# Heads 2 to 6 in couples of seven half products, with the operands kept in DRAM in between

## What is computed

```python
def layer(x, ...):
    h = rmsnorm(x, g_pre_mix)
    z = h @ w_in
    b_g, c_g, xin, cq, ckv_raw, kpe_raw, ga, gb = split(z)
    yc, new_buf = short_conv(c_g * xin, conv_buf, conv_w)
    y_a = b_g * yc
    q = (rmsnorm(cq, g_q) @ w_uq)           # 8 heads, rotary part apart
    y_b = mla_attention(q, latents, rotary keys, w_uk, w_uv)
    merged = sigmoid(ga) * y_a + sigmoid(gb) * y_b
    x = x + rmsnorm(merged @ w_o, g_post_mix)
    f = square(relu(rmsnorm(x, g_pre_ffn) @ w1)) @ w2
    return x + rmsnorm(f, g_post_ffn)
```

## Time and profile before

| | us |
|---|---|
| median of 3 runs | 1749.77 (1749.56 to 1752.14) |
| the profiled execution | 1752.92 |
| its span on the core | 1751.1 |
| TensorE busy in it | 1736.5 (99%) |
| VectorE, ScalarE, GpSimd busy | 1156.4 (66%), 794.3 (45%), 167.9 (10%) |
| mean TensorE clock granted | 0.998 |

### The profile page before, as it was taken

One profiled execution on the slowest core, in us unless ns is written; L12 is line 12 of the kernel. 1 busy time (PEld: TensorE's weight loads), 2 busy tenths in 40 slices (PEclk: granted clock), 3 DMA queues, 4 the chain that ended last, 5 costly groups with the idle time before them and its releaser, 6 DMA issues.

```text
span 1751.1 us, 31636 instructions
## 1 busy us (share of the span) xinstructions
PE 1736.5 (99%) x12975; PEld 1723.4 (98%) x12975; DVE 1156.4 (66%) x2232; ACT 794.3 (45%) x1541; POOL 167.9 (10%) x239
## 2 busy tenths in 40 slices
PE   9999999999999999999999999999999999999998
PEld 9999999999999999999999999999999999999997
DVE  7765555658798566657687555556577886666565
ACT  7634343335465454435366343434345545444452
POOL 0322222000000000000003222222000000000000
PEclk9999999999999999999999999999999999999999
DMA  4688878432213434333227887887513214333331
GB/s 175 174 197 178 192 176 186 106 100 76 86 52 110 131 123 133 121 116 132 74 95 157 168 159 176 148 176 155 135 62 109 74 67 164 120 116 119 126 110 55
DMA packets 83904, 224.57 MB, mean 128 GB/s; under 512 B 9776, under 2 KB 21296, under 8 KB 83760
## 3 DMA queue, kind: packets, MB, share of 16 engines
q1 hardware_dynamic: 57520, 163.82, 28.5%
q0 software_dynamic: 24960, 56.64, 19.3%
q10 hardware_dynamic: 1280, 2.10, 0.4%
HBM read 218.65 MB, written 60.49 MB: 159 GB/s over the span
## 4 chain that ended last, share of the span: by engine, by line
PE 97%; DMA 2%; DVE 1%; ACT 0%; SPq 0%; issue 0%; DVEq 0%
PE ring L720 20%; PE ring L722 20%; PE ring L721 20%; PE att L720 11%; PE att L722 11%; PE att L721 11%; PE att L2992 1%; DMA w_raw<-blocks_in 1%; DMA small_raw<-small_in 1%; PE att L715 1%; PE att L714 1%; PE att L727 0%; PE att L728 0%; PE att L2807 0%; PE att L3048 0%; DVE last L2761 0%
## 5 line engine op out<-in xcount | busy, mean ns | idle before, releaser
L720 PE MATMUL ring<-xs_hi,w_lo 128*128 128x288 f32 x2272 | 674.9, 297 | 0.9 <-issue 0.4
L722 PE MATMUL ring<-xs_hi,w_hi 128*128 128x288 f32 x2272 | 669.2, 295 | 0.0
L721 PE MATMUL ring<-xs_lo,w_hi 128*128 128x288 f32 x2272 | 669.0, 294 | 0.0
L720 PEld LDWEIGHTS ring<-xs_hi,w_lo 128*128 128x128 f32 x2272 | 426.7, 188 | 3.3 <-issue 0.8
L721 PEld LDWEIGHTS ring<-xs_lo,w_hi 128*128 128x128 f32 x2272 | 426.9, 188 | 1.6
L722 PEld LDWEIGHTS ring<-xs_hi,w_hi 128*128 128x128 f32 x2272 | 426.6, 188 | 0.0
L1800 DVE TENSOR_TENSOR w_lo<-w_raw,w_hi 128x1024 fp32r<-128x1024 f32 (+1 forms) x286 | 330.5, 1167 | 73.3 <-ACT w_hi L1270 60.5
L722 PE MATMUL att<-f_hi,w_hi 128*128 128x288 f32 x960 | 283.2, 295 | 0.0
L721 PE MATMUL att<-f_lo,w_hi 128*128 128x288 f32 x960 | 282.9, 295 | 0.0
L720 PE MATMUL att<-f_hi,w_lo 128*128 128x288 f32 x960 | 282.6, 294 | 0.0
L721 PEld LDWEIGHTS att<-f_lo,w_hi 128*128 128x128 f32 x960 | 180.4, 188 | 0.0
(11 more groups left out here) (297 smaller groups left out, 2727.9 us busy)
## 6 DMA issues: line engine op xcount, KB each, us to landing
w_raw<-blocks_in SPq DMA_DIRECT2D x211, 512.0 KB, 4.3
weight_sums<-blocks_in POOLq DMA_DIRECT2D x192, 256.0 KB, 6.8
w_raw<-weight_sums SPq DMA_DIRECT2D x48, 512.0 KB, 3.8
w_raw<-blocks_in SPq DMA_DIRECT2D x26, 256.0 KB, 3.3
weight_sums<-weight_sums POOLq DMA_DIRECT2D x24, 256.0 KB, 6.3
small_raw<-small_in SPq DMA_DIRECT2D x16, 320.0 KB, 4.7
small_raw<-small_in SPq DMA_DIRECT2D x32, 128.0 KB, 5.9
x<-x_in SPq DMA_DIRECT2D x8, 288.0 KB, 6.8
```

The costliest lines, as they stand in the source:

```text
L720: pe.matmul(out, w[1], x[0], start=first, stop=False)
L721: pe.matmul(out, w[0], x[1], start=False, stop=False)
L722: return pe.matmul(out, w[0], x[0], start=False, stop=last)
```

## The change

Heads 2 to 6 ("mixed") no longer make gb, ga, C and x as blocks. C and x form one couple, ga and gb another, each of seven half products (Winograd's form of Strassen, as in the feed-forward couples) over four tiles: x's upper and lower features by both halves of the tokens. B stays a block. A mixed head takes eight slot positions of weights instead of five, two half products each.

For that x is multiplied by its row norm and gain in heads 0 and 1 (`normed_rows`), stored in DRAM (`h_kept`), four differences of it are made over x and `my` (`head_mix`, `head_mix_lo`), and normed x is read back and split in head 2. As `my` is taken, each head's result is stored in `my_kept`, and rows 0 to 6 are read back at head 7, with x (from the input, or in layer 1 from `x_kept`, stored when the layer begins). GpSimd makes the sums of both layers, 44 couples, in one stretch in layer 0, pipelined over four couples.

```diff
+FIRST_MIXED, LAST_MIXED = 2, 6
 # SP
             sp.wait_ge(pl.row_sum, 2 * L + 1)
+            if L > 0:
+                sp.wait_ge(pl.x_new, x_new(L - 1, "post_b", KC - 1))
+                sp.dma_start(pl.x_kept, pl.x[:, :, :]).then_inc(pl.x_spilled, 16)
             sp.dma_start(pl.cos[:, :], tables[0]).then_inc(pl.tables_landed, 16)
             sp.dma_start(pl.sin[:, :], tables[1]).then_inc(pl.tables_landed, 16)
...
+            for h in range(HEADS):
+                if h > 0:
+                    sp.wait_ge(pl.merged, L * HEADS + h)
+                    sp.dma_start(pl.my_kept[:, h - 1, :], my_row(pl, h - 1)).then_inc(pl.my_stored, 16)
+                if h == 1:
+                    sp.wait_ge(pl.h_made, KC * (L + 1))
+                    sp.dma_start(pl.h_kept, pl.x[:, :, :]).then_inc(pl.h_stored, 16)
+                if h == HEADS - 1:
+                    sp.wait_ge(pl.my_stored, stored(L, HEADS - 2))
+                    sp.dma_start(pl.my[:, 0:KC - 1, :], pl.my_kept[:, 0:KC - 1, :]).then_inc(pl.my_landed, 16)
+                    sp.dma_start(pl.x[:, :, :], x_in if L == 0 else pl.x_kept).then_inc(pl.x_back, 16)
+                for j in range(HEAD_POS[h + 1] - HEAD_POS[h]):
+                    if j == (3 if is_mixed(h) else 2):
+                        next_small(h)
...
+                    elif is_mixed(h):
+                        sp.wait_ge(pl.ring_full, full(L, r_mixed(h, (1, 3, 5, 8, 9, 11, 13, 15)[j])))
+                    else:
+                        sp.wait_ge(pl.ring_full, full(L, r_hd(h, j, 1)))
+                    pos_load(HEAD_POS[h] + j + N_HEAD)
 # GpSimd
+        def all_sums():
+            n_sums = DEPTH * (2 * MIXED + PAIRS)
+            sums_copy(0)
+            for n in range(n_sums + 2):
+                if n < n_sums:
+                    pool.wait_ge(pl.sums_copied, 48 * (n + 1))
+                if 1 <= n <= n_sums:
+                    pool.wait_ge(pl.sums_first, 32 * n)
+                if 2 <= n <= n_sums + 1:
+                    pool.wait_ge(pl.sums_second, 16 * (n - 1))
+                if n >= 3:
+                    pool.wait_ge(pl.sums_third, 16 * (n - 2))
+                if n + 1 < n_sums:
+                    sums_copy(n + 1)
+                if n < n_sums:
+                    sums_add_first(n)
+                if 1 <= n <= n_sums:
+                    sums_add_second(n - 1)
+                if n >= 2:
+                    sums_add_third(n - 2)
...
             key_rope(L, 1)
-            for g in range(FIRST_PAIR, GROUPS):
-                for p in range(2):
-                    weight_sums(L, g, p)
+            if L == 0:
+                all_sums()
 # VectorE, a plain head, after the two copies of ga
+                if first:
+                    normed_rows(0, 3)
+                elif h == FIRST_MIXED - 1:
+                    head_mix(0)
+                    head_mix(1)
                 row_maxima(h)
                 absorbed_lo(h, pl.u)
+                if h == FIRST_MIXED - 1:
+                    head_mix(2)
...
                 merge(h, slice(0, NP_), pl.merged)
+                if first:
+                    normed_rows(3, KC)
+                elif h == FIRST_MIXED - 1:
+                    head_mix_lo(2)
+                    head_mix_lo(3)
 # TensorE
+            def mixed_head(h):
+                if h == FIRST_MIXED:
+                    projections(h)
+                for i in range(4):
+                    product(h, 0, i)
+                if h != FIRST_MIXED:
+                    projections(h)
+                for i in range(4, 7):
+                    product(h, 0, i)
+                scores(h)
+                mixed_block(h)
+                turns(h)
+                for i in range(3):
+                    product(h, 1, i)
+                attended(h)
+                for i in range(3, 7):
+                    product(h, 1, i)
```

More of the change, by code:

```diff
@@ L824, in _ @@
                 slot_load(L, n_head(0, i), SLOT_HD[i])
[L825 to L847, removed]
@@ L966, in _ @@
     def _(pool):
[L968 to L986, removed]
@@ L1384, in x_hi_a @@
+            for h in range(HEADS):
+                if is_mixed(h):
+                    mixed_head(h)
+                else:
+                    plain_head(h)
             def x_hi_a(k):
                 if k < HEADS - 1:
[L1386 removed]
+                    eng.wait_ge(pl.my_landed, 16 * (L + 1))
                 else:
@@ new lines, in absorbed_lo, with probabilities @@
+            def absorbed_lo(h, rest):
+                eng.wait_ge(pl.abs_hi, of_head(h, 1, 0))
+                to = slice(64 * h, 64 * (h + 1))
+                rest = rest[:, 0:2 * NS_].rearrange("p (c q) -> p c q", c=CC)
+                own.step(minus(rest, absorbed_tile(pl)[:, :, 0, :], pl.qah[:, :, to]))
+                own.wait()
+                dve.tensor_tensor(pl.qal[:, :, to], absorbed_tile(pl)[:, :, 1, :], rest, ALU.add) \
+                    .then_inc(pl.abs_lo, 1)
+            def probabilities(h):
+                eng.wait_ge(pl.exped, of_head(h, 4, KT - 1))
+                own.step(dve.reciprocal(pl.ri[:, :], pl.rs[:, :]))
+                own.wait()
+                for t in range(KT):
+                    tile = pl.probs[:, PO[t]:PO[t] + P * (t + 1)]
+                    dve.tensor_scalar(tile, tile, pl.ri[:, t:t + 1], None, ALU.mult).then_inc(pl.normed, 1)
@@ new lines, in half_weight, with half_product @@
+            def half_weight(h, n):
+                hi, lo, _ = pl.half_slot(pos_slot(HEAD_POS[h] + n // 2), n % 2)
+                return hi, lo
+            def half_product(idx, weight, x_of, first, last):
+                for k in range(4):
+                    w = slice(k * P, (k + 1) * P)
+                    ins = mm3(pe, pl.ring[:, bank(L, idx), 0:NH], (weight[0][:, w], weight[1][:, w]), x_of(k),
+                              first and k == 0, last and k == 3)
+                return ins
```

1171 lines of the change are left out of this document (785 added, 386 removed).

## The result

The changed kernel took **1902.0 us** (median of 4 runs, 1898.26 to 1913.32), the kernel before 1749.66 beside it: a ratio of 1.088 (95% interval 1.083 to 1.0927), 152 us slower. The forecast was 1758.6 us, between 1732 and 1798. The sign was right, which says little, since the prediction's own chances were 0.49 for slower and 0.40 for faster; the size was off by 143 us. The profiled execution took 1898.26 us, span 1896.4.

What follows compares the result with a forecast made beforehand. TensorE's matmuls were taken as the bound (busy 1736.5 of 1751.1 us). Terms -31.7 + 4.6 + 4 + 6 - 1.1 + 12 + 15 = +8.8 gave 1761.7 us profiled, 1758.6 as median; range 1732 to 1798.

Steps and rivals of the forecast that it cites:

- Removed work: Heads 2 to 6, both layers: couples of seven half products instead of eight remove 240 matmuls, -31.7 us.
- (a): VectorE in a mixed head: about 37 us of 44, staying under TensorE's time, costed at nothing.
- (b): Head 1 of each layer: two differences of x on VectorE ahead of the mask fill, +4.6 us for both.
- (c): Head 2 of each layer: remainders, reloaded normed x and rotary work come together, +4 us for both, bounds 0 and 10.
- (e): Loads beside the sums land late in layer 0's heads 3 to 6, +6 us (0 to 20); layer 1 gains 1.1.
- the faster rival: Loads keep their cover and TensorE stays the bound: 1735 us, between 1728 and 1746; chance 0.36.
- (f): Head 7: reload of result rows and x delays small weights and key cache in layer 0, +12 us (3 to 26).
- (g): Start of layer 1: store of x lengthens the path and key rotation waits behind all sums, +15 us (4 to 45).
- (d): Weight sums on GpSimd: 44 couples, 352 transfers, end at 921 to 972 us, engines about nine tenths full through layer 0.
- the one with the DMA engines as the bound: Rival: DMA engines bound layer 0, sums take until 972 us, 87.5 us of pauses, 1805 us; chance 0.12.
- the bank rival: Half products turn PSUM banks twice as fast, TensorE waits 1 us per couple (20), 1755 us; chance 0.06.

Runs made afterwards that it cites:

- without sums: Changed kernel with all sums of weight blocks left out, plain blocks read instead, so results are not the reference's: 1740.46 us (one run).
- after: The complete changed kernel as first measured, against the kernel before: 1902.0 us median, ratio 1.088.
- the run in two parts: Changed kernel with 32 couples of sums made in layer 0 and the last 12 behind layer 1's key rotation: 1798.66 us median, ratio 1.029.
- The run with less room: Changed kernel with room for GpSimd's queued transfers cut from 1024 to 768 bytes a partition: 1990.64 us.

## Why the prediction was right and wrong, step by step

- **Removed work, -31.7: right.** 240 matmuls fewer. The rate at full clock is the same.
- **(a) VectorE in a mixed head, nothing: right as long as the weights come in time.** Without sums TensorE's waits at products into `ring`, whatever they were for, come to 1.9 us, and to 5.8 in after, not counting one of 1.5 us at the very start that the kernel before has too.
- **(b) head 1, +4.6: right in cause and size.** 2.35 + 2.36 without sums, gone when the calls are moved. In after layer 0's was 5.7, the sums having made the weight block ahead of it late as well.
- **(c) head 2, +4: right.** 3.6 us of pauses in layer 0 (157 to 170 us) and 1.7 in layer 1.
- **(e) late loads, +6: right as far as it went.** 3.0, 2.3 and 1.1 us at 188, 231 and 334 us. But 6.0 us more came in the feed-forward part (1.8, 1.2 and 2.9 at 560, 652 and 843 us), where the sum has no term, though I had written that the engines would be nine tenths full there. That the first sum would be there in time, as the faster rival has it, was wrong: SP stood 17.8 us for it. The 1.1 us of layer 1 are gone, as said.
- **(f) head 7, +12: right in size, and by the reload, but not by the load that I named.** 13.9 us in layer 0, 2.9 in layer 1, where I had nothing. I had the key cache late, ahead of the output projection; ScalarE in fact waited 14.2 us for a weight block behind the reload (issued 388.82, landed 407.62), ahead of the transposes.
- **(g) start of layer 1, +15: wrong, it was 115** (104.2 + 13.2 - 2.4). Its mechanism, the key rotation behind all sums, is what happened, and the run in two parts shows it. The part that I gave to the store of x, 4 us alone and some 11 beside the sums, measures 2.0 without sums (4.3 or 4.4 against 2.4) and 10.8 beside them (13.2 against 2.4): too large alone, right beside the sums. Whose it is stays open, as said above.
- **(d) is the term that failed.** It gave GpSimd's end as 921 to 972 us; it was 1071. I built it from engine time: 352 transfers at 1.40 to 1.69 us of all engines, plus SP's loads, plus 1.5 us idle a round, as if GpSimd's queue got whatever SP leaves free. The run with less room and the round at 1008 us show otherwise. With SP loading nothing, the engines were 0.61 busy and a round still took 21.5 us. The row that had the answer is a start time in the kernel before:

```profile
59.66 0.71 POOL L974 DMA_DIRECT2D weight_sums<-blocks_in  x1
...
300.00 0.83 POOL L974 DMA_DIRECT2D weight_sums<-blocks_in  x1
```

  Eleven couples from the first to the twelfth start: 240.3 / 11 = 21.9 us a couple, with nine transfers and the engines 0.81 busy. 44 x 21.85 from 59.6 on ends at 1021 us, already 93 us past the 928 at which the rotation was due. I took it that eight transfers, with the couples overlapped, would go faster; they took 22.6.
- **What I left out: the clock.** Stretches after long pauses ran below the 2.4 GHz level: the granted clock is 0.86 from 400 to 450 us, 0.66 from 950 to 1000, and 0.50, the 1.2 GHz level, while TensorE did nothing from 1000 to 1050. It is an estimated 16 to 18 of the 20.7 us of busy time in after. The ten transposes took 2.40 us behind the pauses of 13.9, 5.7 and 3.0 us and 1.3 to 1.4 behind those of 2.3. Behind the longest pause matmuls start 0.24 us apart, where 0.132 is the rate at the 2.4 GHz level:

```profile
1080.03 0.44 PE L799 MATMUL att<-cqn_hi,small_hi 128*128 128x288 f32 x1
...
1080.27 0.44 PE L797 MATMUL att<-cqn_hi,small_lo 128*128 128x288 f32 x1
```

  The Trainium skill ("TensorE: Matmul & The Clock Gate", part 1) says that an idle TensorE returns to half clock, and this trace agrees; the prediction named the page and put nothing in the sum.
- **The rivals.** Closest was the one with the DMA engines as the bound, 1805 us, deciding where GpSimd's end passes 950. Its consequence happened with the price 2.4 times too small (43 us late instead of 104), and its cause is not quite it: the engines were not full, GpSimd's queue was slow by itself. The bound of 972 was where the range ended, and it was no bound, since it held no case in which a round has a length of its own. The one in which the loads keep their cover fell: with sums they do not, in after's heads. Of the bank rival's 20 us there are 1.5 in after: waits for a bank that VectorE or ScalarE freed late came to 1.1 us at 334 and 0.4 at 169.
- **The range** took the worst value of one model for the worst case. The other model, elapsed time couple by couple, was one division away.

## What to carry to other kernels

Price a chain of dependent transfers on one queue by the elapsed time of a round, from start to start in the timeline, not by the share of the engines that it uses; and ask what stands behind it on the issuing engine. A step that is needed at a fixed time (here a 7 us rotation) does not go behind background work whose length is only estimated: splitting that work in two gave back 101 of 145 us. Background work that cost little before can cost when the change adds loads and waits of its own: 44 couples cost the kernel before 18 us at most and the changed one 57, so measure the cover that is left, not the cost so far.

## What the runs showed of the hardware

- GpSimd's queue holds only a few transfers. With 1024 bytes a partition of room the fifth transfer of a round waited 4.71 us and the seventh 7.34; with 768 bytes the fourth and the sixth did. Idle of this kind is shown as `issue`, since no semaphore is behind it. In after it came to 262.9 us at one line and 248.1 at another:

```profile
POOL weight_sums L1129 <- issue: 262.9, 42, 8.3
POOL weight_sums L1123 <- issue: 248.1, 42, 13.1
```

- With the copies gone to SP's queue, the fourth addition of nearly each round still waited 5 to 10 us, behind three additions; with the copies, three copies and an addition went out before the first such wait. So fewer additions than copies seem to fit at once.
- The same 44 couples took 22.6 us each over the whole, and 21 us in the stretch without SP's loads: the loads hardly slow the sums, while the sums slow the loads. The median weight block of 512 KB took 3.6 us in the run without sums and 5.1 in after; behind the 4.4 MB reload and beside the sums one took 20.4 us (head 7, the run in two parts).
